# Modulation biases fetched as rows and turned on TensorE, and a square root with an early table in the residual norms

## The reference

```python
def rmsnorm(x, g):
    y = xf * lax.rsqrt(jnp.mean(xf * xf, axis=-1, keepdims=True) + NORM_EPS)
    return (y * g.astype(jnp.float32)).astype(x.dtype)
...
def adaln(cvec, w, b):
    m = jnp.einsum('bd,de->be', jax.nn.silu(cvec), w) + b
    return jnp.split(m[:, None, :], 6, axis=-1)
...
def trunk_layer(x, mods, lp, cache):
    sh1, sc1, g1, sh2, sc2, g2 = mods
    h = rmsnorm(x, lp['norm1']) * (1.0 + sc1) + sh1
    mix, ctx_tensors = token_mixers(h, lp, cache)
    x = x + g1 * mix
    h = rmsnorm(x, lp['norm2']) * (1.0 + sc2) + sh2
    x = x + g2 * moe_ffn(h, lp)
    return x, ctx_tensors
```

## Time and profile before

| what | value |
|---|---|
| time, median of 3 runs | 2104.05 us (2103.68 to 2104.08) |
| profiled execution: its time | 2103.88 us |
| profiled execution: its span, first to last instruction | 2102.1 us |
| PE busy | 1853.3 us, 88% |
| DVE busy | 734.3 us, 35% |
| ACT busy | 569.8 us, 27% |
| POOL busy | 303.9 us, 14% |
| mean granted TensorE clock | 0.94 of full |
| DMA moved | 518.67 MB, mean 247 GB/s |

### The profile page before, as it was taken

One profiled execution on the slowest core, in us unless ns is written; L12 is line 12 of the kernel. 1 busy time (PEld: TensorE's weight loads), 2 busy tenths in 40 slices (PEclk: granted clock), 3 DMA queues, 4 the chain that ended last, 5 costly groups with the idle time before them and its releaser, 6 DMA issues.

```text
span 2102.1 us, 36737 instructions
## 1 busy us (share of the span) xinstructions
PE 1853.3 (88%) x14666; PEld 1039.9 (49%) x14666; DVE 734.3 (35%) x1450; ACT 569.8 (27%) x1170; POOL 303.9 (14%) x372
## 2 busy tenths in 40 slices
PE   3986877778999999999859778888799999999994
PEld 1444676744445444444324357776454454444451
DVE  0033467623422222222220435664423222222222
ACT  1023353422222222222220245533212222222222
POOL 0010132206810000000000102250277000000000
PEclk9998998989999999999979987889799999999997
DMA  8844210044999999999556530001469999999990
GB/s 314 330 155 165 104 67 4 14 179 180 388 386 370 386 382 377 376 381 375 231 208 248 192 109 9 5 2 69 160 268 382 381 377 379 378 385 374 384 366 32
DMA packets 97129, 518.67 MB, mean 247 GB/s; under 512 B 16256, under 2 KB 22016, under 8 KB 40064
## 3 DMA queue, kind: packets, MB, share of 16 engines
q1 hardware_dynamic: 81024, 505.64, 61.7%
q10 hardware_dynamic: 16000, 11.55, 1.8%
HBM read 515.27 MB, written 1.90 MB: 246 GB/s over the span
## 4 chain that ended last, share of the span: by engine, by line
PE 81%; DVE 9%; ACT 3%; issue 2%; ACTq 2%; DVEq 2%; DMA 0%; PEldq 0%; PEld 0%
PE P L1261 21%; PE P L726 20%; PE P L1297 11%; PE P L1243 9%; PE P L1309 8%; PE P L923 5%; DVE PR L1809 3%; DVE W L1809 2%; PE P L752 1%; ACTq L1397 1%; PE P L1281 1%; DVE z L1809 1%; DVE ring L1809 1%; PE P L1226 1%; PE P L1273 1%
## 5 line engine op out<-in xcount | busy, mean ns | idle before, releaser
L1261 PE MATMUL P<-ring,PR 128*64 128x512 f32 x2080 | 457.6, 592 | 2.1 <-DVE PR L2335 1.4
L1261 PEld LDWEIGHTS P<-ring,PR 128*64 128x64 f32 x2080 | 151.4, 137 | 295.3 <-issue 295.3
L726 PE MATMUL P<-ring,hT 128*128 128x512 f32 (+2 forms) x640 | 262.9, 575 | 19.9 <-ACT PR L1696 9.1
L1809 DVE TENSOR_TENSOR PR<-P,PR 128x512 f32<-128x512 f32 (+2 forms) x176 | 107.5, 651 | 402.1 <-ACT PR L1731 375.5
L1297 PE MATMUL P<-W,z 128*64 128x512 f32 x1040 | 237.5, 598 | 2.3 <-ACT z L1722 2.3
L726 PEld LDWEIGHTS P<-ring,hT 128*128 128x128 f32 x640 | 124.1, 207 | 156.7 <-issue 136.6
L1243 PE MATMUL P<-z,PR 128*128 128x128 bf16 x2080 | 178.2, 219 | 0.1
L1731 ACT ACTIVATE PR<-P 128x512 bf16<-128x512 f32 x130 | 70.5, 594 | 366.1 <-PE P L1297 366.1
L1309 PE MATMUL P<-PR,z 128*128 128x512 bf16 x520 | 157.9, 386 | 10.5 <-DVE z L1809 10.5
L1243 PEld LDWEIGHTS P<-z,PR 128*128 128x128 bf16 x2080 | 135.5, 98 | 52.4 <-issue 52.4
L1243 PE MATMUL P<-z 128*128 128x128 bf16 x1040 | 143.0, 219 | 0.0
(11 more groups left out here) (371 smaller groups left out, 2311.3 us busy)
## 6 DMA issues: line engine op xcount, KB each, us to landing
ring<-in_moe_w_gu SPq DMA_DIRECT2D x130, 2048.0 KB, 10.4
W<-in_moe_w_down SPq DMA_DIRECT2D x130, 1024.0 KB, 8.5
ring<-in_ada_w SPq DMA_DIRECT2D x24, 2048.0 KB, 10.5
ring<-in_w_in SPq DMA_DIRECT2D x20, 1024.0 KB, 7.9
ring<-in_w_out SPq DMA_DIRECT2D x4, 2048.0 KB, 8.6
ring<-in_shared_w_gu SPq DMA_DIRECT2D x2, 2048.0 KB, 9.5
ring<-in_w_in SPq DMA_DIRECT2D x4, 672.0 KB, 5.5
PR<-in_gdn_conv ACTq DMA_DIRECT2D x6, 384.0 KB, 12.6
```

The costliest lines, as they stand in the source:

```text
L726: return pe.matmul(out, lhsT, rhs, start=start, stop=stop)
L1261: last = pe.matmul(P[64 * s:64 * s + 64, gb, :], xe[i][:, k, 64 * s:64 * s + 64], v3(ring[s0 + s][:, :], KD)[:, k, :], start=k == 0, stop= ...
L1809: return dve.tensor_tensor(out, p, q, op)
```

## The change

The biases (24 rows of 512) and the norm weights (8 rows of 512) are fetched as contiguous rows into 32 partitions of a free part of `W1`. A new PSUM tile `("biasT",)`, the first of layer 0, takes them turned: PE waits for the identity and the rows and does four transposes, ahead of the first `ada_part`. DVE copies them to their old places ahead of the first norm, instead of waiting for the DMAs before `take_ada(0, 0)`.

In all five residual norms ACT takes `Sqrt` of the sums with the scale 1/D and epsilon as its bias (a constant that POOL writes), and DVE takes the reciprocal. DVE's multiply-add and two semaphores are gone. A one-element `Sqrt` (`root_table`) stands ahead of the wait for `x` in each norm, so that its table can be fetched there. In the second norm of a layer the sum of squares of group 0 waits only for that group's part of `x`.

```diff
 def plan(l):
     t = []
-    t += [(("ada", 0, 0), "A"), (("modT", 0, 0), "V")] * (l == 0)
+    t += [(("biasT",), "V"), (("ada", 0, 0), "A"), (("modT", 0, 0), "V")] * (l == 0)
...
+        bias_rows = W1[0:32, 2560:3072]
...
                 if l == 0:
+                    pe.wait_ge(ident_in, 16)
+                    pe.wait_ge(adab_in, 48)
+                    b = tile(l, ("biasT",))
+                    for k in range(4):
+                        last = pe.transpose(b[:, 32 * k:32 * k + 32], bias_rows.rearrange("r (p k) -> r k p", k=4)[:, k, :],
+                                            cst("ident", 32)[:, 0:32])
+                    last.then_inc(filled, 1)
                     pe.wait_ge(cT_ready, 1)
                     for q in range(4):
                         ada_part(0, 0, q)
-                    pe.wait_ge(ident_in, 16)
                     turn_ada(0, 0)
...
-            act.dma_start(sm["adabT"].rearrange("p (m k) -> p m k", k=4),
-                          a["ada_b"].rearrange("l (m p k) -> p (l m) k", p=128, k=4)).then_inc(adab_in, 16)
+            act.dma_start(bias_rows[0:24, :], a["ada_b"].rearrange("l (m n) -> (l m) n", n=512)).then_inc(adab_in, 16)
             for w, name in enumerate(("norm1", "norm2")):
-                act.dma_start(nT[:, w, :, :].rearrange("p l (h k) -> p (l h) k", k=4),
-                              a[name].rearrange("l (h p k) -> p (l h) k", h=2, k=4)).then_inc(adab_in, 16)
+                act.dma_start(bias_rows[24 + 4 * w:28 + 4 * w, :], a[name].rearrange("l (h n) -> (l h) n", n=512)
+                              ).then_inc(adab_in, 16)
...
+            def root_table():
+                act.activation(sm["root"], sm["eps"], ACT.Sqrt)
+
             for l in range(LAYERS):
                 now[0] = l
+                root_table()
                 act.wait_ge(x_done, l + 1)
...
                     for g in range(2):
+                        if which:
+                            act.wait_ge(empty["V"], tiles.emptied(l, ("out", 1, g)))
                         ins = act.activation(W1[:, 6144:7168] if which == 0 else PR[:, 0:D], x[:, g, :], ACT.Square,
                                              accum_out=sm["ss"][:, g:g + 1])
                         act.drain()
-                        act.nop().then_inc(ss_ready, 1)
-                    act.wait_ge(ss_eps, n)
-                    act.activation(sm["rs"][:, 0:2], sm["ss"][:, 2:4], ACT.Ln)
-                    act.drain()
-                    act.activation(sm["rs"][:, 2:4], sm["rs"][:, 0:2], ACT.Exp, scale=-0.5).then_inc(rs_ready, 1)
+                    act.activation(sm["rs"][:, 0:2], sm["ss"][:, 0:2], ACT.Sqrt, bias=sm["eps"], scale=1.0 / D
+                                   ).then_inc(rs_ready, 1)
...
-                act.wait_ge(empty["V"], tiles.emptied(l, ("out", 1, 1)))
+                root_table()
                 norm(1, l * 2 + 2)
...
             def norm(n):
 
-                dve.wait_ge(ss_ready, n * 2 + 2)
-                dve.tensor_scalar(sm["ss"][:, 2:4], sm["ss"][:, 0:2], 1.0 / D, EPS, ALU.mult, ALU.add
-                                  ).then_inc(ss_eps, 1)
                 dve.wait_ge(rs_ready, n + 1)
+                dve.reciprocal(sm["rs"][:, 2:4], sm["rs"][:, 0:2])
+                dve.drain()
...
-                        dve.wait_ge(adab_in, 48)
                         take_ada(0, 0)
...
+                if l == 0:
+                    name = ("biasT",)
+                    b = f(l, name)[:, 0:128].rearrange("p (k r) -> p k r", k=4)
+                    dve.tensor_copy(sm["adabT"].rearrange("p (r k) -> p k r", k=4), b[:, :, 0:24])
+                    done(dve.tensor_copy(sm["nT"].rearrange("p (r k) -> p k r", k=4), b[:, :, 24:32]), name)
+                    dve.drain()
                 normalise(l * 2, 0, l == 0)
...
+            pool.memset(sm["eps"], EPS)
             pool.memset(sm["cT"], 0.0).then_inc(zeroed, 1)
```

More of the change, by code:

```diff
@@ L290, in build @@
         SP = sb("small_params", 3088)
-        SM = sb("small", 1730)
+        SM = sb("small", 1732)
         most = ctx.enter_context(nc.sbuf_tensor("more_blocks", [128, 1 + 2 * MORE], I32))
@@ L336, in build @@
         for name, w in [("ss", 8), ("rs", 8), ("c16", 16), ("cT", 256), ("modT", 192), ("adabT", 96),
-                        ("nT", 32), ("stage", 512), ("nalog", 8), ("gg", 16),
+                        ("nT", 32), ("eps", 1), ("root", 1), ("stage", 512), ("nalog", 8), ("gg", 16),
                         ("beta", 16), ("t16", 16), ("gcs", 32), ("ngc", 16), ("egs", 32), ("nqk", 16), ("mx", 4), ("sum", 4),
@@ L341, in build @@
             o += w
-        assert o <= 1730
+        assert o <= 1732
         modT = sm["modT"].rearrange("p (l m k g) -> p l m k g", l=LAYERS, m=6, k=KD)
@@ L478, in build @@
         lora_in = sem("lora_in")
-        ss_ready = sem("sum_squares_ready")
-        ss_eps = sem("mean_square_ready")
         rs_ready = sem("rstd_ready")
```

## The result

| | before | after |
|---|---|---|
| time, median | 2104.08 us (2103.66 to 2108.52, 7 runs) | 2086.47 us (2078.19 to 2093.95, 7 runs) |
| ratio of the times | | 0.9909, 95% interval 0.9888 to 0.993 |
| profiled execution, its span | 2103.88, 2102.1 us | 2086.42, 2084.6 us |
| mean granted TensorE clock in it | 0.940 | 0.934 |

The changed kernel is faster, by 17.6 us at the median; the forecast was 2082 with a range of 2076 to 2089.

What follows compares the result with a forecast made beforehand. PE was taken to bound most slices, the change touching gaps between; start 9.9, norms 3.8 + 3.8 + 2.6 + 1.9, together 22.0 us off 2103.88, gave 2082. Own range 2080 to 2085; 8-in-10 range 2076 to 2089.

Steps and rivals of the forecast that it cites:

- What is late next at the start: Start: rows land between 9.7 and 13.4 us, transposes cost at most 1.1; last modulation quarter's landing at 27.1 sets the end.
- slow end: Start, PE at its lower clock: quarter 3.3 us, `w_in` begins at 38.0, 1.7 us lost behind it; gain 8.0 us.
- fast end: Start, PE at full rate: quarter 1.85 us, `w_in` waits for its first piece behind `consts` until 35.9; gain 11.8 us.
- Second norms: Second norm of each layer: one sum of squares and the root remain on the path; 3.8 us saved in each.
- First norm of layer 1: Layer 1's first norm: both sums remain, the root stands where the first table load did; 2.6 us saved.
- Last norm: Final norm: the weight's DMA, 3.7 us from the end of `x`, becomes the last wait; 1.9 us saved, not 2.6.
- Costed at nothing: Early roots hidden ahead of ACT's long waits, 1.5 us each without cover; POOL's constant, PSUM bank shift and sigmoid's table also free.
- (a): Rival: a table load stays in each norm because Square and Sqrt share no table; 4.4 us, 2086.4; chance 0.12.
- (b): Rival at the start: the rows land late, PE gets them only near 32 us, no gain there; 2092; chance 0.05.
- (d): Rival: slower than before, PE holding `ada_part` and `w_in` loads back for late rows; 2108 if landing at 47; chance 0.03.
- (c): Rival: PE's clock stays up at second norms and router, with the start's larger gain; 28.7 us, 2075; chance 0.10.
- The sum: Whole kernel: 22.0 us off the profiled 2103.88, plus some us either way from where PE's lower clock falls.

Runs made afterwards that it cites:

- the second profile: The changed kernel run again, unchanged, beside other kernels: median 2088.1 us over 6 runs, ratio 0.9912 to the kernel before.

## Why the prediction was right, point by point

- **What is late next at the start.** Right: the last quarter's landing (27.35, predicted 27.1) and then its matmuls set the end. The rows came at 12.44, between the bounds of 9.7 and 13.4, and their transposes cost 0.66 against at most 1.1.
- **Its size.** 10.4 against 9.9. I took the middle between a fast and a slow end. The slow end came true nearly everywhere up to `w_in`, which began at 37.36 (slow end 38.0): the narrow transposes, quarters 0 and 1 and the norm's transposes ran at half rate, the last quarter at a mixed 2.52 us. But the 64 matmuls of `w_in` took 27.70 and not 29.40, so the 1.7 us that I charged there weren't lost. `consts` and with it `w_in`'s first piece, which I feared for the fast end, were not the last wait: that was ACT's columns. In the second profile they were, at 35.81 against the 35.9 worked out (in three other kernels at 35.60), and there the 64 matmuls took 29.40. So either execution paid for the lower clock about once, before `w_in` or in it, where the fast end has it nowhere and the slow end in both places. That fits the middle, and nine profiles with this beginning lie at 9.6 to 10.6 us; but I took the middle without working this out, so its closeness is partly luck.
- **Second norms.** 3.78 and 3.80 against 3.8. The root took 0.30 where I had taken Ln's 0.27.
- **First norm of layer 1.** 2.53 against 2.6.
- **Last norm.** 2.22 against 1.9, and by the mechanism named: DVE waits for the weight, which took 3.35 us from the end of `x` instead of 3.7.
- **Costed at nothing.** The early roots are hidden: norms with them lose nothing, and without them each loses 1.27.
- **Rivals.** (a), a table load in each norm, is excluded by the trace, and its price was right: the kernel that has the loads gives up 1.27 us in each norm and 0.95 in the last, 4.8 us against the 4.4 worked out. The time alone would have chosen this rival: the median, 2086.47, is its 2086.4 and lies outside the 2080 to 2085 of the forecast itself. Only the rows decide against it. The reason I gave for its fall went beyond what I cited, which doesn't name Square among the cheap functions; that Square needs no load is what the traces show. The kernel before loads a table twice in each norm, and taking both away gained the full sum; by the Trainium skill, "ScalarE: Activation LUTs", section "Table sets: the hidden batching unit", by which Ln and Exp share a set, it would have been about 4.4 us less. (b) and (d), late rows: they land at 12.4, and delay nothing. (c), the clock stays up: no. The transposes of the second norm stayed at 3.67 behind a pause of 4.22 us, and the router got slower, 5.8 to 7.1 us.
- **The sum.** 22.7 us locally against 22.0. The median moved by 17.6. The 4 to 5 us between are the term that I had only as "some us either way", with a mean of nothing: in untouched stretches the profile shows more time at the lower clock. That term was mis-sized. That the median lies in the stated range owes something to luck, as the range reached that far for rival (a)'s sake. Most of the 5 us last, as the mean of 13 runs shows; where they fall changes: in the first profile the mixers lost 9 us in layer 0 and won 4.7 in layer 1, in the second they lost about 5 and 1. The mean clocks over the single runs fit a lasting part, 0.936 in both groups of the changed kernel against 0.938 to 0.939 in the groups of the kernel before; 0.0025 are 10 us at the lower clock (0.0025 x 2 x 2095), by 0.35 some 4 us. The kernel with the norms only doesn't fit: it falls 3.9 us short at a mean clock of 0.939, that of the kernel before. And of the kernel before there is one profile; layer 0's mixers (134 to 345 us in it) are 4.5 to 8.3 us longer in ten of the 13 others, also in the one that only moves the strided DMAs. Why the lower clock takes more there is open.

## What to carry to other kernels

When a stall at the start goes, look for the next arrival and add the work that must follow it; here that was the last quarter's landing with its matmuls, and the 10 us came out. A table load between two dependent instructions costs its full 1.28 us, and nothing if the engine touches the same table ahead of a long wait. When an edit gains less than its rows say, take the mean of many runs before calling the rest chance. Before a rest is explained, read the granted clock of untouched stretches in both traces, and before a gain is credited to an edit far away, see whether a branch has changed its length.

## What was not expected of the hardware

- Matmuls without use made this kernel faster: two ahead of a wait of 2 us brought 32 router matmuls from 7.1 to 3.8 us.
- A branch costs PE's sequencer under 0.5 or 2 to 3.4 us, and which of the two can change when instructions are added far away; a fetch of 16 KB of instructions runs beside every long one.
- Short runs held ACT's queue for 27.6 us in their issue. Where SP's large loads paused after 30.8 us the biases landed 29.1 us after their issue; where these loads followed one another, the norm weights came 47 us after their issue began (4.62 to 51.45).
- Runs of one and the same kernel of 2.1 ms scatter with a standard deviation of 4 to 7 us (the kernel before and the changed one), with 0.3 to 0.4 us for each us at the lower clock.
